# Rounded weights for the recurrence's projections, and recurrence and merge in one stage

## The reference

```python
def _hgrn_direction(q, f_logit, inp, lb, s0, reverse):
    f = lb + (1.0 - lb) * jax.nn.sigmoid(f_logit.astype(jnp.float32))
    log_f = _heads(jnp.log(f), HG_HEADS, HG_DIM)
    k = _heads(1.0 - f, HG_HEADS, HG_DIM)
    v = _heads(inp, HG_HEADS, HG_DIM)
...
    o, s = _gla_chunkwise(q, k, v, log_f, s0)
...
def _hgrn_readout(o, g_raw, norm_w, dtype):
    g = _heads(g_raw, HG_HEADS, HG_DIM).astype(jnp.float32)
    y = _rmsnorm(o, norm_w) * jax.nn.silu(g)
...
def _merge(y_hg, y_at, gates, w_bh, w_ba, w_o):
    g_hg, g_at = jnp.split(gates, 2, axis=-1)
    mixed = jax.nn.sigmoid(g_hg) * (y_hg @ w_bh) + jax.nn.sigmoid(g_at) * (y_at @ w_ba)
    return mixed @ w_o
```

## Time and profile before

| | |
|---|---|
| profiled execution | 3508.18 us, span 3506.1 us |
| median of three runs | 3507.95 us |
| busy over the span | PE 93%, DVE 54%, ACT 34%, POOL 19% |
| stage `hgrn` | 425.7 to 839.6 us of the span |
| stage `merge` | 839.6 to 1120.1 us |

### The profile page before, as it was taken

The page is one execution under the profiler, slowest core; times in us unless marked ns, Lnnn a source line. Parts: engine busy times, 40 slices in busy tenths (PEclk is TensorE's granted clock), DMA queues, the critical chain, the costliest instruction groups (busy, mean ns, idle before and its releaser), DMA issues. The chain is left out here.

```text
span 3506.1 us, 38398 instructions
## 1 busy us (share of the span) xinstructions
PE 3262.6 (93%) x15060; PEld 2438.4 (70%) x15060; DVE 1879.7 (54%) x2863; ACT 1203.9 (34%) x1878; POOL 653.3 (19%) x616
## 2 busy tenths in 40 slices
PE   7999999998999999999998988987888899999997
PEld 4476554545787878888886866664466678888785
DVE  6546645555233464444476544354765485565558
ACT  3325622223322343333234232542220253333444
POOL 2100000000100045453001010010000025454442
PEclk7999999996999999999999999998989899999998
DMA  5430000001333122224774132233324132232865
GB/s 224 181 132 13 10 25 25 25 1 55 138 97 144 69 85 81 85 87 154 265 297 150 44 100 64 82 116 124 103 72 156 48 114 97 100 113 95 273 228 171
DMA packets 124763, 389.24 MB, mean 111 GB/s; under 512 B 15751, under 2 KB 33159, under 8 KB 109352
## 3 DMA queue, kind: packets, MB, share of 16 engines
q1 hardware_dynamic: 86872, 267.32, 21.9%
q0 software_dynamic: 21056, 111.05, 8.5%
q10 hardware_dynamic: 16656, 8.42, 1.3%
HBM read 312.17 MB, written 74.58 MB: 110 GB/s over the span
## 5 line engine op out<-in xcount | busy, mean ns | idle before, releaser
L1620 PE MATMUL banks<-work,weight_ring 128*128 128x512 f32 (+1 forms) x640 | 265.0, 560 | 5.4 <-ACT x L1710 4.9
L2224 POOL TENSOR_TENSOR quad_raw<-quad_raw 128x512 f32<-128x512 f32 x160 | 233.6, 1461 | 125.1 <-DMA quad_raw<-in_w_gu 118.9
L2356 PE MATMUL banks<-block_t_high,quad_low 128*128 128x512 f32 x608 | 236.6, 389 | 0.0
L1620 PEld LDWEIGHTS banks<-work,weight_ring 128*128 128x128 f32 x640 | 115.9, 190 | 115.0 <-issue 104.5
L2509 ACT ACTIVATE quad_partial<-banks 128x512 f32<-128x512 f32 x160 | 95.6, 598 | 247.0 <-PE banks L2356 236.6
L1820 DVE SCALAR_TENSOR_TENSOR x<-x,work,banks 128x128 f32<-128x128 f32 x320 | 111.3, 348 | 128.3 <-PE banks L1656 119.8
L2354 PE MATMUL banks<-block_t_high,quad_high_b 128*128 128x512 f32 x456 | 177.5, 389 | 0.1
L2355 PE MATMUL banks<-block_t_low,quad_high_b 128*128 128x512 f32 x456 | 177.4, 389 | 0.0
L2356 PE MATMUL banks<-block_b_high,quad_low 128*128 128x512 f32 x456 | 177.4, 389 | 0.0
L3370 PE MATMUL banks<-mix_high,ring_parts 128*128 128x512 f32 x320 | 135.7, 424 | 13.3 <-ACT work L3429 4.4
L2595 DVE TENSOR_TENSOR quad_gated<-banks,quad_partial 128x512 f32<-128x512 f32 x40 | 27.7, 691 | 217.8 <-PE banks L2356 211.2
(11 more groups left out here) (650 smaller groups left out, 8068.1 us busy)
## 6 DMA issues: line engine op xcount, KB each, us to landing
quad_raw<-in_w_gu SPq DMA_DIRECT2D x40, 768.0 KB, 4.2
condition_space<-in_mod_w POOLq DMA_DIRECT2D x24, 1024.0 KB, 7.0
pair_raw<-in_w_down SPq DMA_DIRECT2D x22, 1024.0 KB, 5.1
down_raw<-in_w_down SPq DMA_DIRECT2D x33, 512.0 KB, 4.5
columns_raw<-ffn_blocks SPq DMA_DIRECT2D x33, 512.0 KB, 5.7
weight_ring<-in_w_merge SPq DMA_DIRECT2D x24, 512.0 KB, 3.6
quad_raw<-in_w_gu SPq DMA_DIRECT2D x48, 256.0 KB, 3.0
weight_ring<-in_dft SPq DMA_DIRECT2D x12, 1024.0 KB, 5.1
```

The lines of the kernel that those rows point to most:

```text
L1620: mm = e.matmul(pg.ps[:, bank_of(h, n), 0:b - a], slot[:, (2 * k + t) * P:(2 * k + t + 1) * P], h1[:, k, a:b], start=(k == 0), stop=(k == ...
L2224: e.tensor_tensor(self.weight(n, out), self.weight(n, a), self.weight(n, b), op).then_inc(self.sums.sem, 1)
L2356: mm = e.matmul(bank, w_lo[:, k], hi[:, k], start=False, stop=(k == 3), skip_group_check=again)
```

## The change

1. The projections of the recurrence become rounded products. `w_hgrn` is stored as 16 tiles of 128x1024, and all 40 tiles (16 for the heads, 16 for the merge gates, 8 for the branches) go through one ring, `MergeRing`. ScalarE rounds each; GpSimd takes the low part of tiles 3 to 20, VectorE that of tiles 0 to 2 and of 21 and later.
2. The input `h` is split at the head of the stage (8 tiles of 128x1280), and head 0's six gate fills are made together, tile by tile of the input (`first_gates`).
3. The stages `hgrn` and `merge` become one. The merge gates come first: five of their 32 fills lie beside the last head's steps, the next three follow them, the other 24 come after the head's outputs are turned. Sigmoids go to two staging halves and to DRAM. The branches come last, their inputs brought back from DRAM, where the attention output and each head's output were put; VectorE multiplies straight out of PSUM.
4. The recurrence's values `V` are put in DRAM during the attention stage and brought back head by head, two at a time.

```diff
+class MergeRing:
+    def slot(self, i):
+        return (i + 2) % 3
...
+    def load(self, e):
+        for i in range(self.ALL):
+            if i >= 3:
+                self.used(e, i - 3)
+            e.dma_start(self.pg.ring_raw[self.slot(i)], self.source(i)).then_inc(self.loaded[self.slot(i)].sem, 16)
...
 def hgrn(pg):
...
     def pool(e):
...
+        for h in range(HEADS):
+            ring.take_low(e, 4 * h + 4)
+            if h:
+                e.wait_ge(done, h)
+                e.dma_start(pg.branches_dram[3 + h], G[:, (h - 1) % 2, :]).then_inc(pg.heads_kept[(h - 1) % 2].sem, 16)
+                if h + 1 < HEADS:
+                    next_values(h + 1)
+            for n in range(1, 5 if h + 1 == HEADS else 4):
+                if h + 1 == HEADS:
+                    mg.store(e, n - 1)
+                ring.take_low(e, 4 * h + 4 + n)
...
     def tensor(e):
+        def product(h, n, k):
+            part, (t, a, b) = fills[n]
+            i = 4 * h + 2 * part + t
+            if k == 0:
+                ring.split.wait(e, i + 1)
+            w_hi, w_lo = (v[:, k * P:(k + 1) * P] for v in ring.parts(i))
+            bank = pg.ps[:, bank_of(h, n), 0:b - a]
+            e.matmul(bank, w_hi, pg.h1_high[k][:, a:b], start=(k == 0), stop=False)
+            e.matmul(bank, w_hi, pg.h1_low[:, k, a:b], start=False, stop=False)
+            mm = e.matmul(bank, w_lo, pg.h1_high[k][:, a:b], start=False, stop=(k == KT - 1))
...
-                slot = pg.weights(e, g0 + 2 * h + part)
-                mm = e.matmul(pg.ps[:, bank_of(h, n), 0:b - a], slot[:, (2 * k + t) * P:(2 * k + t + 1) * P],
-                              h1[:, k, a:b], start=(k == 0), stop=(k == KT - 1))
+                product(h, n, k)
+
+        def first_gates():
+            for k in range(KT):
+                e.wait_ge(h_split, k + 1)
+                for n in range(FG):
+                    product(0, n, k)
...
                 if h + 1 < HEADS:
                     project(h + 1, beside[s])
+                else:
+                    merge_gate(s // 4, range(2 * (s % 4), 2 * (s % 4) + 2))
             if h + 1 < HEADS:
                 project(h + 1, all_of([FG + 1]))
+            else:
+                merge_gate(5, range(4, KT))
+                for p in (6, 7):
+                    merge_gate(p, range(KT))
             turn_outputs(h)
...
     def scalar(e):
+        ring.take_high(e, 0)
+        input_high(0)
+        ring.take_high(e, 1)
+        for k in range(1, KT):
+            if k == 3:
+                e.wait_ge(pg.v_kept, 64)
+            input_high(k)
+        ring.take_high(e, 2)
...
         store(0, range(FG))
+        ring.take_high(e, 3)
         gate_logs(0)
         for h in range(HEADS):
+            ring.take_high(e, 4 * h + 4)
...
 def merge(pg):
     def tensor(e):
+        for p in range(mg.IN_HEAD, GA):
...
+            for k in range(KT):
+                mg.product(e, p, k)
+        for n in range(KT):
+            i = ring.GATES + n
             split.wait(e, i + 1)
+            for q in range(4):
+                br, s = 1 - q // 2, q % 2
+                p = GA + 4 * n + q
+                read.wait(e, p - 7)
...
-    pg.stage(name="merge", sync=sync, gpsimd=pool, tensor=tensor, scalar=scalar, vector=vector)
+    pg.stage(name="merge", gpsimd=pool, tensor=tensor, scalar=scalar, vector=vector)
+    pg.together("hgrn_merge", 2)
```

More of the change, by code:

```diff
@@ L1762, in vector, with input_low @@
         ch = pg.vchain(e)
+        def input_low(k):
+            e.wait_ge(h_high, k + 1)
+            e.tensor_tensor(pg.h1_low[:, k, :], h1[:, k, :], pg.h1_high[k].bitcast(F32), ALU.subtract).then_inc(h_split, 1)
+        ring.take_low(e, 0)
+        input_low(0)
+        ring.take_low(e, 1)
+        for k in range(1, KT):
+            input_low(k)
+        ring.take_low(e, 2)
         tables.wait(e, 32)
+        e.wait_ge(pg.branches_kept, 64)
         ch(e.memset(SM, 0.0))
@@ L1856, in merge @@
 def merge(pg):
-    BR, GA, N = 4 * KT, 4 * KT, 3 * KT
-    h1, x = pg.h1, pg.x
+    ring, mg = pg.merge_ring, pg.merge_gates
+    GA, HG = 4 * KT, ring.HGRN
+    x = pg.x
+    high, split, full, read = ring.high, ring.split, ring.full, ring.read
     mixed_high, mixed_low = pg.h_parts
-    y = Mem(pg.big, M_YAT, M_W1)(KT, T)
-    staging = Mem(pg.big, M_W1 + KT * T, M_END)(4, HALF)
-    m = Mem(pg.big, M_YAT, M_W1)
+    y = Mem(pg.big, M_X, M_H)(KT, T)
+    m = Mem(pg.big, M_H, M_YAT)
     B, sg = m(2, 2, T), m(2, 4, HALF)
-    dram = pg.scratch_dram("branches", KT, P, 2, T)
@@ L1872, in merge @@
     again = pg.sem("x_loaded_again")
-    loaded = [pg.shared_sem(f"projection_loaded_{n}", 16 * len(range(n, N, 3))) for n in range(3)]
-    high, split, full, read = (pg.shared_sem(f"projection_{n}", c) for n, c in (
-        ("high", N), ("split", N), ("full", BR + GA), ("read", BR + GA)))
     y_high, y_split = pg.shared_sem("norm_high", KT), pg.shared_sem("act_split", KT)
-    h_high, h_split = pg.sem("merge_input_high"), pg.sem("merge_input_split")
-    stored = [pg.sem(f"branch_stored_{n}") for n in range(4)]
@@ L1894, in sync @@
-    def sync(e):
-        e.wait_ge(pg.stage_done, 3 * k_merge)
-        for i in range(N):
-            first, n_pieces, n, cols = item(i)
-            if i >= 3:
-                at, count = item(i - 3)[0:2]
-                full.wait(e, at + count)
-            e.dma_start(pg.ring_raw[i % 3], w[n][:, cols]).then_inc(loaded[i % 3].sem, 16)
-    pg.merge_ring_0_used = lambda e: full.wait(e, sum(item(N - 3)[0:2]))
-    pg.merge_full = lambda e: full.wait(e, BR + GA)
-    def pool(e):
-        for p in range(BR):
-            n, q = divmod(p, 4)
-            br, s = divmod(q, 2)
-            read.wait(e, p + 1)
-            e.dma_start(dram[n, :, br, half(s)], staging[:, p % 4, :]).then_inc(stored[p % 4], 16)
-        for slot in range(4):
-            e.wait_ge(stored[slot], 16 * KT)
+    back = pg.sem("branch_inputs_loaded")
@@ new lines, in merge @@
+    gates = [pg.sem(f"branch_loaded_{n}") for n in range(2)]
+    summed, mix_high, mix_split = (pg.sem(f"merge_{n}") for n in ("summed", "high", "split"))
+    half = lambda s: slice(s * HALF, (s + 1) * HALF)
+    Y_EARLY, Y_AFTER, FIRST_LOW = 3, 20, 21
+    pg.merge_ring_0_used = lambda e: ring.used(e, ring.ALL - 3)
+    pg.merge_full = lambda e: ring.used(e, ring.ALL - 1)
+    def pool(e):
+        for p in range(mg.IN_HEAD, GA):
+            mg.store(e, p)
+            if p == mg.IN_HEAD:
+                for kept in pg.heads_kept:
+                    kept.wait(e, 32)
+                e.wait_ge(pg.hgrn_done, 4)
+                for k in range(KT):
+                    e.dma_start(y[:, k, :], pg.branches_dram[k]).then_inc(back, 16)
+        for slot in range(2):
+            mg.stored[slot].wait(e, 16 * GA // 2)
+        full.wait(e, GA)
@@ new lines, in tensor @@
+        for p in range(mg.IN_HEAD, GA):
+            if p == 9:
+                read.wait(e, 7)
+            elif p == 11:
+                read.wait(e, 8)
+            elif p >= 12:
+                read.wait(e, p - 3)
+            for k in range(KT):
+                mg.product(e, p, k)
+        e.wait_ge(pg.hgrn_done, 4)
+        for n in range(KT):
+            i = ring.GATES + n
+            split.wait(e, i + 1)
+            w_hi, w_lo = ring.parts(i)
+            for q in range(4):
+                br, s = 1 - q // 2, q % 2
+                p = GA + 4 * n + q
+                read.wait(e, p - 7)
+                bank = pg.ps[:, p % 8, :]
+                for k in range(4):
+                    j = 4 * (1 - br) + k
+                    if n == 0 and s == 0:
+                        y_split.wait(e, j + 1)
+                    at = slice((4 * br + k) * P, (4 * br + k + 1) * P)
+                    e.matmul(bank, w_hi[:, at], pg.y_high[:, j, half(s)], start=(k == 0), stop=False)
+                    e.matmul(bank, w_hi[:, at], pg.y_low[:, j, half(s)], start=False, stop=False)
+                    mm = e.matmul(bank, w_lo[:, at], pg.y_high[:, j, half(s)], start=False, stop=(k == 3))
@@ L1955, in tensor, with take @@
                 mm.then_inc(full.sem, 1)
     def scalar(e):
[L1958 to L1961 removed]
+        def take(k):
+            if k == 0:
+                e.wait_ge(back, 16 * KT)
+            e.activation(pg.y_high[:, k, :], y[:, k, :], ACT.Copy).then_inc(y_high.sem, 1)
         def mixed(n, s):
```

330 lines of the change are left out of this document (191 added, 139 removed).

## The result

| | before | changed |
|---|---|---|
| runs | 3503.49 to 3509.79 us (4) | 3455.27, 3440.89, 3451.64, 3454.01 us |
| median | 3507.24 us | 3452.82 us |
| profiled execution | 3508.18 us, span 3506.1 us | 3455.27 us, span 3453.4 us |

The ratio is 0.985, 95% interval 0.983 to 0.987: 54 us faster. Forecast were 3446.6 us and 3433 to 3470. The time lies in the range, 6 us above the forecast; the profiled execution is 8.7 us above it.

What follows compares the result with a forecast made beforehand. PE's own work was taken as the limit, except in the half-clock last head and an idle gap behind it. From 3508.18 us, -5.3 - 12.0 + 5.4 - 49.7 = -61.6 gave 3446.6 us, range 3433 to 3470.

Steps and rivals of the forecast that it cites:

- start to T0 of head 0: From the stage's start to head 0's first turn (T0): 62.0 us before, T0 at 482.3 instead of 487.7, -5.3 us.
- The 256-column pass: Rounded pass of 256 columns, absent from the trace: taken at 0.12 us, so 0.36 us per k.
- weight loads bound the 256-column passes: Rival: 256-column passes take 0.19 to 0.227 us, the weight load's length; +13 to +20 us, 3460 to 3467; chance 0.13.
- a 256-column rounded pass costs a whole fp32 product: Rival, as worded: 0.43 us each, 60 us more, 3507 us, no change; chance 0.03.
- The step: A middle step of a head's recurrence shortens from 3.45 to 3.10 us; steps T0 to T19 together -6.4 us.
- the step does not get shorter: Rival: the chain of turn, copy, update and four state steps takes over; 21 us more, 3468 us; chance 0.08.
- Between heads: From T19 of one head to the next head's T0: 34.2 us before, 35.4 forecast, +1.2 us.
- The lock: VectorE and GpSimd share a port pair, so GpSimd's subtraction of tile 4h+4 lengthens the preparation between heads by 2.4 us.
- The clock: PE's idle stretches bring 3.4 us at half clock: 1.5 us added at the start, 1.2 at each head.
- The last head and the seam: Last head's T0 to T19 rises 5.4 us to 55.8; from its T19 to the last pass -49.7 us, to 242.4.
- one fifth the cheaper product: Split of the forecast gain: four fifths from the last head and the seam, one fifth from the cheaper rounded product.
- The ring starves PE: Rival: PE waits for weight tiles from three slots, 7.2 us each; 20 waits give 3591 us, slower; chance 0.03.

Runs made afterwards that it cites:

- the earlier rounding: Changed kernel with ScalarE rounding the next head's weight tile 4h+4 before its last square of the norm, not behind the root: 3449.66 us, 0.985 of before.
- VectorE's own subtraction: Outputs scaled behind the first scan, query fill out of steps 20 and 21, plus tile 4h+4 subtracted by VectorE instead of GpSimd: 3429.97 us, 0.979 of before.
- the kernel with fp32 products: Changed kernel with the recurrence's projections as one fp32 product per k again, new order and ring kept: 3474.94 us, 0.991 of before.
- the kernel with both edits: Changed kernel with outputs scaled behind the next head's first scan and the query fill moved out of steps 20 and 21: 3438.73 us, 0.980 of before.

## Why the prediction was right

The sum against the profiled execution, term by term:

| term | forecast, us | measured, us | error |
|---|---|---|---|
| start to T0 of head 0 | 56.6 | 58.7 | +2.1 |
| heads 1 to 3, T0 to T0 | 91.2 | 91.9 | 3 x 0.7 |
| last head, T0 to T19 | 55.8 | 56.9 | +1.1 |
| T19 to the last pass | 242.4 | 241.9 | -0.5 |
| last pass to the stage's end | 4.3 | 2.7 | -1.6 |
| behind the stage | 2386.1 | 2391.8 | +5.7 |

The errors add up to 8.9 us, for the 8.7 of the profiled execution; the difference is rounding.

- **The 256-column pass**: taken at 0.12 us, measured 0.12. The rivals "weight loads bound the 256-column passes" and "a 256-column rounded pass costs a whole fp32 product" fall.
- **The step**: 3.10 forecast, 3.13 to 3.18 measured. Without half clock T0 to T19 is 55.2 us where my terms give 54.6. PE stays the limit; the rival "the step does not get shorter" falls. The pass in the steps starts every 0.23 us.
- **Between heads**: 35.4 forecast, 35.3 measured. The lock was taken at 2.4 us; the scan went from 2.82 to 5.00, 2.2. The first scan, the tile and the mechanism were right; the earlier rounding and VectorE's own subtraction show it by two ways of removing it. In head 0 the same lock was taken at 3.3 us beside the scans, and there it was wrong: both scans took 2.82, the first subtraction fell into VectorE's idle time, and the second stretched the `tensor_scalar` between the scans (0.80 us elsewhere):

```profile
469.04 2.97 DVE L2008 TENSOR_SCALAR x<-x 128x1280 f32<-128x1280 f32 x1
```
```profile
468.40 2.93 POOL L1582 TENSOR_TENSOR ring_parts<-weight_ring,ring_parts 128x1024 fp32r<-128x1024 f32 x1 [2.23 <-ACT ring_parts L1576]
```

  From the gate fills' end to T0 it was 23.4 us, against 23.5 forecast, by luck: 1.1 us too much for the lock stood against tile 3, for whose load ScalarE waited 0.6 us and which it rounded in 1.06 us ahead of its Ln, 1.7 where I had 0.9. (The three parts that I named, 19.1, 0.9 and 3.3, add up to 23.3.)
- **The clock** was the term that was most mis-sized. I had 3.4 us at half clock behind each idle time, from the one case in the trace, a price of 1.5 us at the start and 1.2 per head. The rows show 6.8 us at the start and 6.8 us around T0, of which 3.1 lie under the steps. In the steps it cost 1.4 us (56.6 against 55.2), so 1.2 was near. At the start, profiles with 3.4 us at half clock have 52.9 to 53.1 us from the first pass to T0, those with 6.8 have 54.3 to 54.5, and my step had 52.5. Of the error of 2.1 us about 1.4 is that second stretch, 0.4 the first pass (430.2, not 429.8). That head 0's steps, too, come to 56.6 us is luck: PE was idle only 0.9 us ahead of that T0, and the stretch of 3.4 us began 6 us behind it.
- **The last head and the seam**: -49.7 forecast, -50.2 measured. The gates out of the last head show that PE's passes account for it. I had missed that the passes in this head also lift the clock of the fills behind it: with the gates taken out, the half clock reaches 10.7 us beyond T19.
- **The split of the gain**: "one fifth the cheaper product" is wrong, and already my own terms gave more (12.0 + 5.3 of 61.6, 28%). The product alone is worth 24 of the 59 us in the stage, two fifths. My step set the new order's costs (lock, splits) against the product in one sum per head, -4.0, and the sum was right to 0.7 us; its parts were not told apart.
- **The ring starves PE**: no sign of it. PE waited for no weight tile behind T0 of head 0; ScalarE waited 7.9 us for six tiles of the merge, ahead of need:

```profile
  DMA weight_ring<-in_w_merge: 7.9, 6
```

- **Behind the stage** lies the largest single error, 5.7 us, in unchanged code. The two profiles of the same changed kernel have 2391.8 and 2392.7 us, but with edits inside the stage only it was also 2382 to 2394. That variation goes in part with the granted clock: the three shortest (2382.0, 2383.0 and 2385.3 us) have 177 to 185 us at half clock there, the two of the changed kernel 199 and 200; but profiles with 196 to 199 us lie anywhere between 2385.6 and 2393.5. The kernel before has 198, so against it the clock explains little: PE is busy 1.3 us longer, and the other 4.4 us are PE's idle time. Whether the change causes them stays open; there is one profile of the kernel before, and no experiment aimed at it.

## What to carry to other kernels

Work that has no dependence on a latency-bound recurrence is nearly free beside it: 27.5 us of passes cost 6 us in the last head, where the granted clock rose with them from 0.50 to 0.97. Where a helper engine takes a task off VectorE, look at what VectorE does at that moment; the subtraction that GpSimd made cost VectorE's chain 2.2 us, and 1.2 when VectorE made it. Shorten a chain between two PE-bound parts until PE's idle time is gone, not by half. T0 to T19 of heads 1 to 3 together took 170.3 and 171.5 us with 6.7 us of idle time ahead of T0, 173.3 to 173.8 with 3.7 to 5.1, and 165.7 to 168.8 with 1.4 or less: half-way the half clock moved onto the steps and took back part of the gain. Some half clock in a head's first steps stays even then, so profile a kernel more than once before 2 or 3 us are credited to an edit.

## What the runs showed of the hardware

- Half clock: with PE idle from 569.7 us, the granted clock fell at 572.8 and rose at 579.6, 3.2 us after PE had begun again. A head without it takes 55.2 us from T0 to T19; with 2.8 to 3.8 us of it in the steps 56.4 to 56.9, with 6.8 to 7.0 us 58.1 to 58.4. In the kernel with the earlier rounding a second stretch of 3.4 us came 9 us behind T0 (59.0 us); PE had been busy for 1.67 of the 3.3 us ahead of it.
- With PE idle for 1.4 us or less ahead of T0 (heads 1 to 3 in five profiles), half clock lay across T0 in none of 15 heads, and a stretch of 3.4 us came 6 to 12 us behind it in 6.
- Such a stretch is not wholly set by the kernel: two profiles of the changed kernel have 6.8 and 3.4 us at the first gate fills, and T0 to T19 of head 0 at 56.6 and 55.2 us.
- In the kernel with fp32 products PE idled only 1.8 us between heads, and no half clock lay between 431 and 1083 us.
- A `tensor_scalar` with one SBUF tensor input (0.94 us) took 3.03 us behind GpSimd's subtraction, and GpSimd's took 3.07 us where it began behind VectorE's (3.43 in the kernel with both edits), against 2.37 in the steps.
